# Gate panels moved in behind each head of a linear-attention stage, level scores computed in half the columns, and a weight ring of three

## The chip, the cores and the metric

The kernel runs on one core of a Trainium2 chip. The metric is the device time of one execution in microseconds (us), the median of several runs. The engines are named as in the profile: PE is TensorE's matrix multiplication and PEld its weight loads, DVE is VectorE, ACT is ScalarE, POOL is GpSimd, and SP is the queue that issues the transfers.

## What is computed

Three transformer-like layers over 512 positions of width 1024, all in float32. The first layer is the one that the change touches. Cut to what matters:

```python
proj = rmsnorm(x, norm_mix) @ w_in
zu, zv, zq, zf, zi, zo, g_a, g_b = jnp.split(proj, split_points, axis=-1)
y_a = gmlp_branch(zu, zv, ...) @ w_up_a          # GELU(u) * (W_s LN(GELU(v)) + b)
y_b = hgrn2_branch(zq, zf, zi, zo, ...) @ w_up_b # gated linear attention, 8 heads of 128
mix = sigmoid(g_a) * y_a + sigmoid(g_b) * y_b
x = x + mix @ w_out
x = x + square(relu(rmsnorm(x) @ w_ff1)) @ w_ff2
```

Inside `hgrn2_branch` each head needs, within every chunk, the scores of query t and key s with a decay between them: `scores = einsum('bhtk,bhsk,bhtsk->bhts', qb, kb, decay)` for s <= t. Then follow a short-convolution layer with its feed-forward block (`ffn_0`), keys and values, attention with 16 heads and a forget bias, and a second feed-forward block (`ffn_1`).

## The kernel before

Every activation lies transposed, features on the 128 partitions and the 512 positions in the free dimension, in tiles of 128x512. Every weight matrix is cut into panels of 128 output features: 353 panels of 128x1024 floats, in one long list whose order is `COUNTS` (L32): zu, zv (4 each), ga (8), upa (8), heads (32), gb (8), upb (8), out1 (8), ff1 (64), and so on. `START` holds where each name begins.

**A panel's way.** SP loads panel p into `w_raw`. ACT rounds it into `w_hi` (`high`, L400, a CAST), POOL subtracts the two into `w_lo` (`low`, L317), and PE multiplies (`product`, L1269): three matmuls of 512 columns for each of eight 128-row tiles (L1284, L1285, L1286: high times high, high times low, low times high), 24 in all, summed in bank p % 2 of PSUM. DVE takes the bank out (mostly `scale_out`, L786). The three buffers are rings of `RING` = 4 panels. ACT issues the rounding three panels ahead of the product that it stands beside (`p + 3`), and both ACT and POOL wait until the product that used the same ring place is made (`made`). A product waits for its `w_low` and for the eviction of the panel two before it.

**Order.** Each engine's program is written out by hand; engines meet through semaphores alone. The gMLP branch comes first: zu, zv, then the eight ga panels with the transposes of zv (`turn_zv`, L1308) and the layer norm (`layer_norm`, L843) beside them, then the mixing matmuls (L1324), then the eight upa panels, which have only four 128-row tiles each (12 matmuls). Then come the heads, then gb, upb, out1.

**A head.** `head(h, a)` stands once on each engine, and works on the four panels of head h (forget, query, value, output gate) and on the attention of head a = h - 1. On PE (L1392) the four products are cut in halves, and between them lie `turns` (transposes and the diagonal products, L1330), `levels` (four calls), `chunk_kv`, `outputs`, and at the end `output_sums` (L1388), which waits until ACT has squared the outputs (L528). The scores within a chunk are built level by level: seven levels, half lengths 64 to 1, each a product of the decayed tile `qk` with itself. `levels(c, a)` makes all seven 128x128 products of one chunk into two banks (L1361). DVE multiplies them and the diagonal by 0/1 masks (`mask_chunk`, L880, three instructions), and POOL adds the eight parts in three steps (`chunk_scores`, L330: L333, L335, L339), from one buffer `masked` that the four chunks share. DVE also forms the decays (`span`, L904, L914 and L915), ACT exponentiates them (L521, L525, L531), POOL multiplies the keys in (`decay_keys`, L342) and DVE the queries (`decay_queries`, L917, L922). Before the sums come the rounding of a panel or two on ACT and their subtraction on POOL.

Most repeated parts are hardware loops (`Fori`): heads 1 to 7, ff1, the convolution and feed-forward pairs, the attention pairs. Waits inside them compare a semaphore with a register, and in the attention loop the keys and values of the pair are copied to fixed places first (`k_now`, `v_now`), and DVE writes a mark (L1197) before each maximum.

Of the kernel before, what the change touches and what calls it, by code (L numbers as in the profile page):

```python
# [8 lines left out]
P = 128  # L9
# [18 lines left out]
ARENA = 17424  # L28


RING = 4
COUNTS = [("zu", 4), ("zv", 4), ("ga", 8), ("upa", 8), ("heads", 32), ("gb", 8), ("upb", 8), ("out1", 8),  # L32
          ("ff1", 64), ("conv_b", 8), ("conv_ch", 16), ("out2", 8), ("ffn_0", 68), ("k", 8), ("v", 8),
          ("f", 1), ("qg", 16), ("out3", 8), ("ffn_1", 68)]
START, N_PANELS = {}, 0
for _name, _n in COUNTS:
    START[_name] = N_PANELS
    N_PANELS += _n
# [4 lines left out]
for _name, _n in [("ident", P), ("ones", P), ("halves", P), ("minus", P), ("neg", P), ("reset", SEQ),  # L43
                  ("levels", LEVELS * P), ("onehot", HEADS_A), ("eps", 1)]:
    CONST_COLS[_name] = (_at, _n)
    _at += _n
# [16 lines left out]
HID_GMLP, HID_HEADS, HID_MIX, HID_FF1, HID_CONV, HID_FFN0, HID_ATTN, HID_FFN1 = 0, 4, 12, 20, 52, 60, 82, 90  # L63


class Steps:

    def __init__(self, eng, sem):  # L70
        self.eng, self.sem, self.n, self.offset = eng, sem, 0, 0
# [6 lines left out]
    def wait(self):  # L78
        self.eng.wait_ge(self.sem, self.n + self.offset)

    @contextmanager
    def loop(self, first, end, marks):
        before = self.n
        with self.eng.Fori(first, end) as i:
            self.offset = (i - first) * marks
            yield i
        self.offset = 0
        assert self.n - before == marks, f"the body marks {self.n - before} steps, not {marks}"
        self.n = before + (end - first) * marks


def tile_at(buf, i):

    if isinstance(i, int):
        return buf[:, i, :]
    return buf[:, bass.ds(i, 1), :].rearrange("p a n -> p (a n)")


def column(buf, i, rows=P):
    return buf[0:rows, i:i + 1] if isinstance(i, int) else buf[0:rows, bass.ds(i, 1)]  # L100


def build(nc, xT, panels, const, param, rows, ws, outT):
# [5 lines left out]
    with ctx:  # L109
# [16 lines left out]
        hid_lo = sb("hid_lo", [P, DT, SEQ], R)  # L126
        consts = sb("consts", [P, N_CONST])
# [3 lines left out]
        wait_mark = sb("wait_mark", [P, 1])  # L131
# [8 lines left out]
        def gain(name, i=0):  # L140
            a, _ = PARAM_COLS[name]
            return column(params, a + i)
# [3 lines left out]
        def take(*shape):  # L146
# [18 lines left out]
        zu, zv = take(GROUPS, SEQ), take(GROUPS, SEQ)  # L165
        vn = take(BLK, SEQ)
        rows_sb = take(3, SEQ)
        ws_sb = take(GROUPS, P)
        ln_stats, ln_mv = take(BLK, 6), take(BLK, 2)
        ln_root, ln_inv = take(BLK), take(BLK)  # L170

        used[0] = after_y
        qk = take(2 + LEVELS, SEQ)
        masked = take(LEVELS + 1, P)

        at = used[0]
        z, za, g, cum = take(SEQ), take(SEQ), take(SEQ), take(SEQ)
        q, k, vT, silu_o = take(SEQ), take(SEQ), take(SEQ), take(SEQ)
        gb = arena[:, at:used[0]].rearrange("p (a n) -> p a n", a=DT)
# [33 lines left out]
        k_now, v_now, key_bias, o_all = take(SEQ), take(SEQ), take(SEQ), take(SEQ)  # L213
# [19 lines left out]
        dve_steps, act_steps, pool_steps = sem("dve_steps"), sem("act_steps"), sem("pool_steps")  # L233
# [10 lines left out]
        level_made, level_masked, scores_done, kv_made, states_done = (sem(n) for n in (  # L244
            "level_made", "level_masked", "scores_done", "kv_made", "states_done"))
# [7 lines left out]
        k_squared, k_normed, v_copied, v_flat, v_spread = (sem(n) for n in (  # L253
            "k_squared", "k_normed", "v_copied", "v_flat", "v_spread"))
        l_abs, l_log, l_done, picked, biased, bias_read = (sem(n) for n in (
            "l_abs", "l_log", "l_done", "picked", "biased", "bias_read"))
        k_loaded, v_loaded, scored, maxed, exped, scaled, turned_p, copied_even, copied_odd, attended, attn_read = (sem(n) for n in (
            "k_loaded", "v_loaded", "scored", "maxed", "exped", "scaled", "turned_p", "copied_even", "copied_odd", "attended", "attn_read"))
# [16 lines left out]
        def _(sp):  # L275
            def load(i, j):
                sp.dma_start(w_raw[:, j, :], panels[i * RING + j]).then_inc(w_in[j], 16)

            sp.dma_start(params[:], param).then_inc(param_in, 16)
            for m in range(DT):  # L280
                sp.dma_start(x[:, m, :], xT[m]).then_inc(x_in[m], 16)
                if m == 0:
                    load(0, 0)
            load(0, 1)
            sp.dma_start(consts[:], const).then_inc(c_in, 16)
            for j in range(2, RING):
                load(0, j)
            sp.dma_start(rows_sb[:, :, :], rows.partition_broadcast(P)).then_inc(row_in, 16)
            sp.dma_start(ws_sb[:, :, :], ws).then_inc(row_in, 16)
            with sp.Fori(1, N_PANELS // RING) as i:  # L290
                at = sp.snap(i * RING)
                for j in range(RING):
                    src = panels[bass.ds(at + j, 1)].rearrange("a p n -> p (a n)")

                    sp.wait_ge(w_low, i * RING + (j - RING + 1))
                    sp.dma_start(w_raw[:, j, :], src).then_inc(w_in[j], 16)
# [1400 lines left out]
```

## Time and profile before

| | |
|---|---|
| runs | 2279.59, 2282.51, 2283.90 us; median 2282.51 us |
| the profiled execution | span 2280.2 us, 28102 instructions |
| DVE, ACT and POOL busy | 1053.0, 803.4 and 1023.1 us |
| idle of PE before L1292 | 55.1 us, 46.7 of them ended by ACT L528 |
| transfers | 353 panels of 512 KB, 3.5 us to land each; 84 GB/s on average |

The profiled execution is 2.3 us shorter than the median of the runs: the span counts from the first to the last instruction. A busy row says how long an engine had something in it. The chain of the page follows the work that ended last backwards, from each instruction to what released it. A window of the trace gives each engine's busy time between two moments counted from the start of the span, with the clock that TensorE was granted as a share of its full 2.4 GHz. Windows below begin at the first matmul of a stage's first product.

### The profile page before, as it was taken

How to read it: one execution, taken by the hardware profiler on the slowest of the kernel's cores; microseconds unless marked ns; L12 is line 12 of the kernel's file. 1: busy time of each engine (PE TensorE's matmuls, PEld its weight loads, DVE VectorE, ACT ScalarE, POOL GpSimd, SP SyncE). 2: the span in 40 equal slices, each digit the busy share in tenths (PEclk: the TensorE clock that was granted, in tenths of full speed). 3: DMA queues.
4: the chain of work that ended last, by engine and by line, in shares of the span. 5: the costliest groups of instructions: out<-in, count | busy, mean ns of one | idle time of the engine just before them, and what ended most of it. 6: DMA issues, size and time to landing. Idle time of an engine off the chain costs nothing.

```text
span 2280.2 us, 28102 instructions
## 1 busy us (share of the span) xinstructions
PE 2178.6 (96%) x9662; PEld 1748.7 (77%) x9662; DVE 1053.0 (46%) x1683; ACT 803.4 (35%) x1141; POOL 1023.1 (45%) x517
## 2 busy tenths in 40 slices
PE   6988887889999999999999999999899999999999
PEld 5876766778788888888788888877666668888887
DVE  3348888862432232434455252531455444625343
ACT  4334435433422222532332222253455544222222
POOL 3457777774344444444444444453311113444443
PEclk9999998999999999999999999999899999999999
DMA  5231111123233332232333233332211002232322
GB/s 186 93 111 47 46 55 46 46 65 93 93 93 94 100 101 92 92 102 84 101 93 101 93 97 97 92 115 80 74 37 36 29 28 93 92 103 91 102 92 93
DMA packets 53779, 192.44 MB, mean 84 GB/s; under 512 B 5968, under 2 KB 6096, under 8 KB 53584
## 3 DMA queue, kind: packets, MB, share of 16 engines
q1 hardware_dynamic: 53712, 191.51, 26.7%
q8 instruction: 46, 0.75, 0.1%
q14 instruction: 21, 0.17, 0.0%
HBM read 189.39 MB, written 2.10 MB: 84 GB/s over the span
## 4 chain that ended last, share of the span: by engine, by line
PE 81%; DVE 9%; issue 4%; POOL 3%; ACT 2%; DMA 0%; SPq 0%; POOLq 0%; DVEq 0%; ACTq 0%
PE ps L1284 25%; PE ps L1286 25%; PE ps L1285 25%; DVE arena L914 2%; PE ps L1515 2%; PE ps L1538 2%; POOL arena L333 2%; POOL w_lo L317 1%; PE ps L1292 1%; DVE arena L915 1%; DVE arena L786 1%; DVE arena L922 1%; DVE arena L908 1%; DVE arena L1117 0%; PE ps L1517 0%
## 5 line engine op out<-in xcount | busy, mean ns | idle before, releaser
L317 POOL TENSOR_TENSOR w_lo<-w_raw,w_hi 128x1024 fp32r<-128x1024 f32 x353 | 851.1, 2413 | 1167.7 <-ACT w_hi L400 1154.9
L1284 PE MATMUL ps<-x_hi,w_hi 128*128 128x512 f32 x1864 | 758.2, 407 | 17.9 <-POOL w_lo L317 9.3
L1285 PE MATMUL ps<-x_lo,w_hi 128*128 128x512 f32 x1864 | 735.0, 394 | 0.0
L1286 PE MATMUL ps<-x_hi,w_lo 128*128 128x512 f32 x1864 | 734.9, 394 | 0.0
L400 ACT CAST w_hi<-w_raw 128x1024 fp32r<-128x1024 f32 x353 | 366.5, 1040 | 346.6 <-PE ps L1286 345.1
L1284 PEld LDWEIGHTS ps<-x_hi,w_hi 128*128 128x128 f32 x1864 | 357.1, 192 | 99.3 <-issue 14.2
L1285 PEld LDWEIGHTS ps<-x_lo,w_hi 128*128 128x128 f32 x1864 | 356.9, 191 | 81.7 <-issue 9.4
L1286 PEld LDWEIGHTS ps<-x_hi,w_lo 128*128 128x128 f32 x1864 | 355.5, 191 | 76.4
L786 DVE TENSOR_TENSOR arena<-ps,inv_rms 128x512 f32<-128x512 f32 x232 | 160.0, 690 | 479.2 <-PE ps L1286 455.6
L1284 PE MATMUL ps<-hid_hi,w_hi 128*128 128x512 f32 x896 | 354.2, 395 | 13.5 <-DVE hid_lo L815 13.2
L1285 PE MATMUL ps<-hid_lo,w_hi 128*128 128x512 f32 x896 | 351.9, 393 | 0.0
L1286 PE MATMUL ps<-hid_hi,w_lo 128*128 128x512 f32 x896 | 351.5, 392 | 0.0
L1284 PEld LDWEIGHTS ps<-hid_hi,w_hi 128*128 128x128 f32 x896 | 170.2, 190 | 53.5 <-DVE hid_lo L815 15.3
L409 ACT ACTIVATE hid_hi<-arena 128x512 fp32r<-128x512 f32 (+1 forms) x112 | 70.0, 631 | 385.0 <-DVE arena L1117 136.8
L1286 PEld LDWEIGHTS ps<-hid_hi,w_lo 128*128 128x128 f32 x896 | 170.2, 190 | 35.9
L1285 PEld LDWEIGHTS ps<-hid_lo,w_hi 128*128 128x128 f32 x896 | 170.5, 190 | 35.1
L815 DVE TENSOR_TENSOR hid_lo<-arena,hid_hi 128x512 fp32r<-128x512 f32 (+1 forms) x112 | 79.2, 712 | 77.4 <-ACT hid_hi L409 77.3
L1134 DVE TENSOR_TENSOR x<-x,ps 128x512 f32<-128x512 f32 x40 | 27.5, 687 | 162.4 <-PE ps L1286 162.4
L643 ACT ACTIVATE arena<-arena 128x512 f32<-128x512 f32 x44 | 27.8, 632 | 211.2 <-DVE arena L1083 211.2
L1292 PE MATMUL ps<-arena,consts 128*128 128x512 f32 x62 | 39.9, 732 | 55.1 <-ACT arena L528 46.7
L1117 DVE TENSOR_TENSOR arena<-arena 128x512 f32<-128x512 f32 x44 | 82.7, 1880 | 4.3
L352 POOL TENSOR_TENSOR arena<-arena 128x256 f32<-128x256 f32 x56 | 63.4, 1164 | 26.5 <-ACT arena L525 26.5
(159 smaller groups left out, 1678.1 us busy)
## 6 DMA issues: line engine op xcount, KB each, us to landing
w_raw<-in_panels SPq DMA_DIRECT2D x353, 512.0 KB, 3.5
x<-in_xT SPq DMA_DIRECT2D x8, 256.0 KB, 4.9
outT<-x SPq DMA_DIRECT2D x8, 256.0 KB, 2.0
consts<-in_const SPq DMA_DIRECT2D x1, 1032.5 KB, 8.4
arena<-in_rows SPq DMA_DIRECT2D x1, 768.0 KB, 11.1
arena<-in_ws SPq DMA_DIRECT2D x1, 256.0 KB, 11.4
params<-in_param SPq DMA_DIRECT2D x1, 112.0 KB, 2.1
```

The lines of the kernel that those rows point to most:

```text
L317: nc.gpsimd.tensor_tensor(w_lo[:, j, :], w_raw[:, j, :], w_hi[:, j, :].bitcast(F), ALU.subtract).then_inc(w_low, 1)
L333: steps.done(nc.gpsimd.tensor_tensor(masked[:, 0:4, :], masked[:, 0:4, :], masked[:, 4:8, :], ALU.add))
L352: nc.gpsimd.tensor_tensor(lv, lv, kv, ALU.mult).then_inc(keys_decayed, 1)
L400: nc.scalar.copy(w_hi[:, j, :], w_raw[:, j, :]).then_inc(w_high, 1)
L409: return nc.scalar.activation(dst, src, ACT.Copy, scale=1.0 if scale is None else scale)
L786: return v.tensor_tensor(dst, bank(p_int), inv_rms[:, :], ALU.mult)
L815: v.tensor_tensor(tile_at(hid_lo, m), src, tile_at(hid_hi, m).bitcast(F), ALU.subtract).then_inc(hid_low, 1)
L1117: v.tensor_tensor(conv_o[:, j, :], conv_u[:, j, :], conv_t[:, j, :], ALU.mult).then_inc(hid_raw, 1)
L1284: nc.tensor.matmul(o, wh, hi[:, kt, :], start=(kt == 0), stop=False)
L1285: nc.tensor.matmul(o, wh, lo[:, kt, :], start=False, stop=False)
L1286: ins = nc.tensor.matmul(o, wl, hi[:, kt, :], start=False, stop=(kt == tiles - 1))
L1292: nc.tensor.matmul(ps[:, bank_n, :], weights, src, start=True, stop=True).then_inc(sums_ready, 1)
```

## The change

- **Loops written out.** No `Fori` is left; all waits are on constants. `k_now`, `v_now` with their copies and waits, and the mark before each maximum, go.
- **Order of the panels.** The eight ga panels and the eight gb panels no longer stand before and behind the heads. `FILL` puts two panels behind the four of heads 1 to 4, one behind heads 5 and 6, two behind head 7, and the last four gb panels are the products of the pass that finishes head 7. upa follows after the heads.
- **The gMLP work** (transposes, layer norm, mixing) moves into head 0, its rounding (`split_gmlp`, `low_gmlp`) into head 1, into buffers of its own (`gm_hi`, `gm_lo`). Before the first turns PE waits until DVE has read the mixed tiles. The sigmoids of ga and gb move to upa and upb.
- **Level scores.** A call of `levels` makes one group of levels for all four chunks, and only the columns of the later halves: 64 instead of 128 moving columns. The number of matmuls stays at 28 a head. DVE copies them into `scores` (cleared once), the first level plainly, the others and the diagonal under a mask with `copy_predicated`: eight copies and four marker instructions a head. POOL's twelve additions a head go, and so do the twelve mask multiplications.
- **Ring of three**, with `FEED` = 2: rounding and subtraction run two panels ahead. The memory freed holds the new buffers; gb lies in `x`, which is loaded again during upb.
- `silu_o` has two buffers, and its eviction comes ahead of the gating of the head before it.

```diff
+RING = 3
+FEED = 2
+FILL = {1: [("ga", 0), ("ga", 1)], 2: [("ga", 2), ("ga", 3)], 3: [("ga", 4), ("ga", 5)],
+        4: [("ga", 6), ("ga", 7)], 5: [("gb", 0)], 6: [("gb", 1)], 7: [("gb", 2), ("gb", 3)],
+        8: [("gb", 4), ("gb", 5), ("gb", 6), ("gb", 7)]}
...
+            for h in range(HEADS_H):
+                p = AT["heads", 4 * h]
+                low(p + 2)
+                low(p + 3)
+                pool.wait_ge(decays_done, h * 4 + 1)
+                decay_keys(h, [0])
+                low(p + 4)
+                pool.wait_ge(decays_done, h * 4 + 2)
+                decay_keys(h, [1, 2, 3, 4])
+                low(p + 5)
+                pool.wait_ge(decays_done, h * 4 + 3)
+                decay_keys(h, [5, 6, 7])
+                for e in range(len(FILL.get(h, []))):
+                    low(p + 6 + e)
...
+            def take_levels(gr, a):
...
+                for at, n in enumerate(LEVEL_GROUPS[gr]):
...
+                    if n == 0:
+                        ins = v.tensor_copy(scores[0:half, :, half:P],
+                                            got[0:half, :].rearrange("p (b n) -> p b n", b=BLK))
+                    else:
...
+                        ins = v.copy_predicated(dst, mask.unsqueeze(1).broadcast_to([P, BLK, P // (2 * half), half]),
+                                                got.rearrange("p (b s h) -> p b s h", b=BLK, h=half))
+                    link(ins)
...
+                v.engine_nop().then_inc(level_taken, 1)
...
+                        ins = nc.tensor.matmul(ps[0:rows_, 4 + gr % 2, to:to + P // 2], lv[:, 0:rows_], later,
+                                               start=True, stop=True)
...
             def turns(a):
...
+                if a > 0:
                     pe.wait_ge(sums_read, a + (R_HEAD))
+                else:
+                    pe.wait_ge(mixed_read, GROUPS)
...
             def head(h, a):
...
+                if h == 0:
+                    for b in range(BLK):
+                        turn_zv(b)
...
+                if h == 0:
+                    mix()
+                fill = FILL.get(h, []) if h is not None else []
+                if fill:
+                    product(p + 4, x_hi, x_lo)
                 if a is not None:
                     output_sums(a)
...
+                for e in range(1, len(fill)):
+                    product(p + 4 + e, x_hi, x_lo)
```

## Rows read from the trace of the kernel before

**Rows 1.** The page: busy time, share of the span and instructions of each engine.
```profile
PE 2178.6 (96%) x9662; PEld 1748.7 (77%) x9662; DVE 1053.0 (46%) x1683; ACT 803.4 (35%) x1141; POOL 1023.1 (45%) x517
```

**Rows 2.** The page's chain of work that ended last, by engine.
```profile
PE 81%; DVE 9%; issue 4%; POOL 3%; ACT 2%; DMA 0%; SPq 0%; POOLq 0%; DVEq 0%; ACTq 0%
```

**Rows 3.** Windows: ga, upa, heads, gb, ff1, attention; PE, PEld, DVE, ACT, POOL, clock, DMA.
```profile
68.09:119.75 51.66, 49.37 (x241) 41.09 (x240) 22.51 (x33) 16.91 (x22) 19.43 (x8) 1.00 0.29 92
119.75:149.28 29.53, 25.02 (x97) 19.43 (x98) 10.62 (x16) 11.48 (x12) 18.13 (x8) 0.88 0.37 108
149.28:475.57 326.29, 272.67 (x1420) 225.54 (x1419) 268.08 (x389) 144.23 (x201) 234.71 (x175) 0.92 0.17 55
475.57:532.61 57.04, 57.04 (x288) 47.83 (x286) 21.60 (x37) 21.98 (x32) 35.87 (x27) 0.97 0.21 65
...
623.65:972.72 349.07, 349.07 (x1539) 288.68 (x1538) 104.35 (x151) 105.89 (x129) 151.53 (x65) 1.00 0.31 97
...
1622.42:1851.77 229.35, 223.69 (x862) 143.70 (x863) 119.15 (x410) 121.91 (x257) 40.09 (x17) 0.95 0.12 39
```

**Rows 4.** Windows: head 0, and head 5, one of seven alike.
```profile
149.28:174.28 25.00, 21.92 (x98) 17.83 (x96) 14.94 (x19) 10.09 (x14) 12.16 (x6) 1.00 0.35 107
...
347.48:389.93 42.45, 35.33 (x192) 29.30 (x190) 36.16 (x54) 19.07 (x28) 31.59 (x25) 0.94 0.16 49
```

**Rows 5.** Timeline of PE in head 5, between the products; last, after its wait.
```profile
354.39 0.60 PE L1335 MATMUL ps<-consts,arena 128*128 128x128 f32 x4
...
360.37 1.73 PE L1361 MATMUL ps<-arena 128*128 128x128 f32 x14
...
388.84 2.08 PE L1292 MATMUL ps<-arena,consts 128*128 128x512 f32 x2 [6.67 <-ACT arena L528]
```

**Rows 6.** A window right behind that wait.
```profile
390.50:396.50 6.00, 6.00 (x20) 4.63 (x19) 5.82 (x7) 3.32 (x7) 5.79 (x7) 0.70 0.00 0
```

**Rows 7.** Timeline of DVE in head 5.
```profile
359.80 1.65 DVE L937 TENSOR_TENSOR arena<-arena 128x512 f32<-128x512 f32 x1
...
378.85 2.60 DVE L914 TENSOR_TENSOR arena<-arena 128x256 f32<-128x256 f32 x1
...
385.61 0.41 DVE L914 TENSOR_TENSOR arena<-arena 128x256 f32<-128x256 f32 x1
```

**Rows 8.** Timeline of POOL in head 5.
```profile
359.24 1.66 POOL L333 TENSOR_TENSOR arena<-arena 128x512 f32<-128x512 f32 x1 [0.63 <-DVE arena L890]
...
378.61 2.56 POOL L317 TENSOR_TENSOR w_lo<-w_raw,w_hi 128x1024 fp32r<-128x1024 f32 x1
...
388.38 7.91 POOL L352 TENSOR_TENSOR arena<-arena 128x256 f32<-128x256 f32 x7 [3.31 <-ACT arena L525]
```

**Rows 9.** Groups of DVE's instructions by line and shape, 149.28 to 510.40.
```profile
L914 DVE TENSOR_TENSOR arena<-arena 128x256 f32<-128x256 f32 x56 | 59.3, 1059 | 0.0
...
L886 DVE TENSOR_TENSOR arena<-ps,consts 128x512 f32<-128x512 f32 x32 | 21.9, 684 | 51.7 <-POOL arena L339 31.3 <-PE ps L1361 20.4
L888 DVE TENSOR_TENSOR arena<-ps,consts 128x384 f32<-128x384 f32 x32 | 17.5, 545 | 0.0
...
L890 DVE TENSOR_TENSOR arena<-ps,consts 128x128 f32<-128x128 f32 x32 | 8.9, 278 | 0.0
```

**Rows 10.** Timeline of the weight loads in attention, at full clock.
```profile
1711.25 0.29 PEld L1515 LDWEIGHTS ps<-arena 64*128 64x128 f32 x2 [0.76 <-issue]
```

**Rows 11.** Timeline at panel v 3: POOL's subtraction, PE's first matmul.
```profile
1577.27 2.40 POOL L317 TENSOR_TENSOR w_lo<-w_raw,w_hi 128x1024 fp32r<-128x1024 f32 x1 [8.66 <-ACT w_hi L400]
...
1581.21 0.48 PE L1284 MATMUL ps<-x_hi,w_hi 128*128 128x512 f32 x1
```

**Rows 12.** Timeline of DVE and PE at the layer norm and the mixing.
```profile
112.73 2.04 DVE L847 TENSOR_TENSOR arena<-arena 128x512 f32<-128x512 f32 x1
...
115.63 3.81 PE L1324 MATMUL ps<-arena 128*128 128x128 f32 x32 [1.99 <-DVE arena L848]
```

**Rows 13.** Timeline of ACT behind the last head.
```profile
514.55 1.28 ACT L554 ACT_TABLE_LOAD   x1
```

More of the change, by code:

```diff
@@ L78, in wait @@
     def wait(self):
[L79 to L100, printed above, removed]
+        self.eng.wait_ge(self.sem, self.n)
 def build(nc, xT, panels, const, param, rows, ws, outT):
@@ L1119, in pair @@
                         low_hid(m + (hid0 + t0 + 1), m, conv_o[:, j, :])
-                    pair(0, 0)
-                    pair(1, 1)
-                    with steps.loop(1, size // 2, 4) as i:
-                        for j in range(2):
-                            pair(i * 2 + j, j)
                     p0 += 2 * size
@@ L1268, in _, with product @@
         def _(pe):
-            def product(p, p_int, hi, lo, tiles=DT, ready=None, done=None, part=None):
-                j = p_int % RING
+            def product(p, hi, lo, tiles=DT, ready=None, done=None, part=None):
+                j = p % RING
                 part = part or (0, tiles)
@@ L1301, in linear @@
                 for m in range(n):
-                    product(p0 + m, p0 + m, hi, lo, tiles, ready if m == 0 else None, done)
+                    product(p0 + m, hi, lo, tiles, ready if m == 0 else None, done)
                     if m == 0 and stream is not None:
@@ L1392, in head @@
             def head(h, a):
-                p, p4 = S["heads"] + 4 * h if h is not None else S["gb"], S["heads"]
-                product(p, p4, x_hi, x_lo)
+                p = AT["heads", 4 * h] if h is not None else AT["gb", 4]
+                product(p, x_hi, x_lo)
+                if h == 0:
+                    for b in range(BLK):
+                        turn_zv(b)
                 if a is not None:
@@ L1413, in head @@
                     outputs(a)
-                product(p + 3, p4 + 3, x_hi, x_lo, part=(4, DT))
+                product(p + 3, x_hi, x_lo, part=(4, DT))
+                if h == 0:
+                    mix()
+                fill = FILL.get(h, []) if h is not None else []
+                if fill:
+                    product(p + 4, x_hi, x_lo)
                 if a is not None:
                     output_sums(a)
-            head(0, None)
-            with pe.Fori(1, HEADS_H) as h:
-                head(h, h - 1)
+                for e in range(1, len(fill)):
+                    product(p + 4 + e, x_hi, x_lo)
@@ L1422, in _ @@
+            for h in range(HEADS_H):
+                head(h, h - 1 if h > 0 else None)
             head(None, HEADS_H - 1)
[L1423 removed]
+            linear(S["upa"], DT, gm_hi, gm_lo, gm_low, 0, tiles=GROUPS)
             linear(S["upb"], DT, hid_hi, hid_lo, hid_low, HID_HEADS)
             linear(S["out1"], DT, hid_hi, hid_lo, hid_low, HID_MIX)
[L1428 removed]
+            for ch in range(FF1_CHUNKS):
                 p0 = S["ff1"] + 16 * ch
[L1430 to L1436 removed]
@@ L1447, in _ @@
                     sums(6, c("ones"), sum_sq_2[:, :])
[L1448 to L1450 removed]
+            linear(S["conv_ch"], 2 * DT, x_hi, x_lo, None, None)
             linear(S["out2"], DT, hid_hi, hid_lo, hid_low, HID_CONV)
```

734 lines of the change are left out of this document (322 added, 412 removed).

## Prediction

> **What bounds the kernel now.** I read the page first. PE is busy 96% of the span [rows 1]; the chain that ended last runs through PE for 81% and through DVE for 9% [rows 2]. So most of the kernel is PE at its pace, and the question is where it is not. The windows by stage answer that [rows 3]. In ff1 64 panels take 349.07 us, 5.45 each; I use 5.44, the pitch from product to product in a quiet stretch, as the price of a full panel. Four hardware loop edges lie in or beside that stage and PE is never idle in it. The heads, 32 panels, take 326.29 us where 32 x 5.44 would be 174; attention takes 229.35 for 16. For the change the stretch from ga to gb counts: 51.66 + 29.53 + 326.29 + 57.04 = 464.5 us.
>
> A head takes 42.45 us with PE busy 35.33 and DVE busy 36.16 [rows 4], and seven heads look alike (42.3 to 43.8). PE stands for 6.67 us before the sums, waiting for ACT L528 [rows 5], which waits for DVE's spans. Behind that wait the granted clock of the window is 0.70 [rows 6]: part of it at the lower level, 1.2 GHz, after 6.67 us in which PE did nothing; product 389.93 spans about 2.5 us more than one at full clock. So the heads are bound by DVE, with POOL and ACT in turn with it, and PE has room there.
>
> Why DVE is that full: its L914 takes 0.41 us alone, but 2.60 while POOL's L317 runs, and both end together; L937 takes 1.65 beside POOL's L333, again ending with it [rows 7, 8]. L914's 56 instructions sum to 59.3 us, where 56 x 0.41 would be 23 [rows 9]. An instruction of DVE with two inputs from on-chip memory waits for POOL's to end. Taking all lines of the heads so, about 11 of DVE's 36 us a head are such waits, and DVE alone would need 25. The Trainium skill ("SBUF — State Buffer", on who interferes with whom) says the same as an exclusive lock in which the loser fully blocks; the common end times here agree. That rule speaks against this change, which hangs one or two more of POOL's subtractions on each head; the third rival prices it from the rows.
>
> **The change part by part.**
>
> *PE's own work in a head.* Four products 21.8; seven transposes, and four diagonal products of two instructions each, all at 0.11, 0.8 + 0.9; levels 28 x 2 instructions at 0.11 (14 in 1.73 us, the last one's own 0.28 taken off, is 0.112) = 6.2; chunk_kv 0.7; outputs 1.5; sums 0.9; changeovers about 0.5. Sum 33.3 us [rows 5].
>
> *Level scores at 64 columns.* The count of matmuls stays, so the price per instruction decides. The trace has no matmul of 64 columns. Two weight loads of 0.18 us each start 0.11 us apart [rows 10], and the transposes of L1335, single instructions where L1361 has two for one product, also come at 0.11 (4 in 0.60) [rows 5]. That looks like a floor set by the weight load, not by the columns streamed. Bounds: nothing saved, or half, 3.1 us a head. I take nothing. In a sentence of its own: the Trainium skill ("TensorE: Matmul & The Clock Gate", LDWEIGHTS) prices a load by its columns, 128 / 1.2 = 107 ns, whatever is streamed behind it, which would give the same zero, against 25 us over eight heads if the streamed columns ruled; the 0.11 us start to start agrees.
>
> *DVE and POOL in a head.* Out go the twelve mask products: L886 0.68, L888 0.55, L890 0.28, four times, 5.4 us with their overlap taken off [rows 9]; and twelve additions on POOL, about 12 us. In come eight copies. The nearest rows are the mask products, which read the same memory: 0.68 for 512 columns, and 0.42 for 256, midway between 0.28 for 128 and 0.55 for 384 [rows 9]: 7 x 0.42 + 0.68 = 3.6, plus 0.1 of waiting behind each = 4.5. A masked copy isn't in the trace; if it took twice the time per element it would be 3.6 more. DVE's waits behind the vanished additions (L937, L944, L964, L908) were 3.4. Each fill panel adds an eviction of 0.7 and a subtraction of 2.4 that can block DVE for up to 2.2. DVE: 36.2 - 5.4 + 4.5 - 3.4 = 31.9, with one fill 33 to 35, with two 34 to 38.
>
> *Fill panels.* PE then needs 33.3 + 5.44 = 38.7 us with one, 44.2 with two. I laid the four queues beside each other with the durations above. With PE's first product at 0, the last levels end at 22; DVE's q, spans and evictions run to 30 to 32; the output squares are done by 31, before PE comes to the sums at 38, since the first fill product now lies where it stood idle; POOL finishes the keys at 40 to 42 and the next head's levels want them at 46 (one fill) or 51 (two). The tightest points are the subtraction of the panel after next (done 36.5 to 38.5, wanted at 38.7 with one fill, 41 to 43 against 44.2 with two) and silu_o's eviction (35 to 37.6 against 38.7). So PE becomes the bound and its clock stays at 2.4 GHz; I add 0.5 us a head for those points. Heads 1 to 7 with twelve fills: 7 x 33.8 + 12 x 5.44 = 301.9 us.
>
> *Head 0* took 25.00 [rows 4] and now carries the gMLP. DVE's statistics 3.6, four norms of 2.2 with one or two blocked like L847 (2.04 for 0.69) [rows 12] 10, before it may evict panel 1, at 23 us; PE wants to start panel 3 at 18, idle 5. Then mixing, 3.6 [rows 12], to 34, the next product to 39.5; but the first turns now wait for the mixed tiles to be read, and those reads (4 x 1.4) stand on DVE behind spans, queries and evictions, done at 46 to 48. Another 7 us idle, and after each stall some time at half clock, 3 us in all. Head 0 costs 45 us (40 to 52).
>
> *The last pass* (gb 4 to 7 and head 7): 34 us. *upa* behind it: 8 x 2.73 = 21.8, plus a wait for its third panel: the rounding stands behind root, gating, split, a table load of 1.28 [rows 13] and a sigmoid, done about 9.5 us after the sums where PE wants it at 5.5: 25.8 us. Bounds 22 to 31.
>
> *Sum.* 45 + 301.9 + 34 + 25.8 = 406.7 against 464.5: 57.8 us less.
>
> *Ring of three, feed of two*, everywhere else. `high(p + 2)` with a ring of three waits for the same product as `high(p + 3)` with a ring of four, and stands at the same place of ACT's queue. So every rounding, subtraction and load keeps its moment and serves a panel one earlier: the margin of a panel is its start less the end of the subtraction now made for the panel behind it. I took that for all panels. It is 1.54 us in v (1577.27 + 2.40 against 1581.21) [rows 11], about the smallest there is outside the stretch already costed; it is never negative there. Cost nothing; if loads or POOL fell 2 us later, half a microsecond for each of some 60 panels, 30 us.
>
> *Loads of x again* on SP hold a panel's load until an eviction, about 2.5 us, with over 5 us to spare: nothing. *Attention*: PE is busy 223.69 of 229.35 [rows 3], so what goes from ACT and DVE (two copies a pair, 64 marks) was hidden: nothing, bounds -6 to 0. *Loops*: ff1 shows no idle time at their edges: nothing, bounds -5 to +10 for the longer code.
>
> Against the profiled execution: 2280.2 - 57.8 = 2222.4; the median lies 2.3 above the span, so 2224.7, say 2225 us.
>
> **The rivals.** (1) The forecast, PE bounds the heads: 2225, its own range 2212 to 2238. (2) The 64 columns do save: 25 us, of which DVE lets about 20 through: 2205. For: nothing but the column count; against: [rows 10]. (3) Slower: DVE and POOL take turns fully. DVE alone 25.5 and POOL 6 x 2.4 + 1.5 + 7 x 0.75 = 21.2 (seven took 7.91 beside DVE [rows 8], 1.13 each, of which about 0.4 was DVE's turn) are 47 us with two fills, 44 with one; with the 6 us that DVE now idles for others, 53 and 50, so 5 x 53 + 2 x 50 = 365, 63 us more than forecast: 2288; with masked copies at double price 2317. I take 2300. It decides once heads 1 to 7 average over 51.4 us, (301.9 + 57.8) / 7. Against: POOL's and DVE's busy times overlap now for most of a head, 36.16 + 31.59 in 42.45 [rows 4]. (4) The tail of a head misses its tight points by 3 to 4 us each: 25 more, 2250. For: margins of 0 to 2 us. (5) The ring starves later stages: 2255. (6) The longer code stalls its engines: the change is not what it says; 2240. (7) Head 0 and attention give more than I grant: 2195.
>
> **How the numbers follow.** Chances: (1) 0.50, (2) 0.14, (3) 0.06, (4) 0.17, (5) 0.05, (6) 0.03, (7) 0.05. The predicted time is that of (1). The range 2198 to 2256 takes in (2), (4), (5) and (6), leaving out (3), (7) and the ends of (4). A measurement of this kernel can tell about 0.2%, 4.6 us, from no change. Slower by more than that is (3) and what I may have overlooked, 0.07; within it 0.03, from a (3) or (4) that meets the old time; faster 0.90.
>
> **What the profile after would show.** Heads 1 to 4 near 44 us and 5 and 6 near 39, clock 1.0, no wait above 1 us before the sums; L1361's successor at 0.11 us per instruction; head 0 near 45 with two stalls of 5 and 7 us; DVE below 38 us a head; subtractions ending before their products everywhere else. It would be wrong if the fills show idle time behind POOL's subtraction or DVE's eviction, if a masked copy takes well over 0.5 us, or if v and the feed-forward stages leave 5.44 us a panel.

## The result and the profile after

The changed kernel takes 2240.56 us (median; runs 2239.78 to 2241.88) where the kernel before took 2282.26 beside it. The ratio is 0.9819, 95% interval 0.9805 to 0.9833: 41.7 us less, where 57.8 were forecast. The time lies within the range on record, 15.6 us above the predicted 2225. Span to span it is 2280.2 to 2238.0, 42.2 us.

Some short names are used below. The *stretch* is ga, upa, heads and gb together, 464.5 us before; in the changed kernel it runs from head 0 to the end of upa. A *fill* is a gate panel whose product stands behind the four products of a head. The *sums* are the two matmuls of `output_sums`, the *spans*, *queries* and *keys* are the instructions of `span` and `decay_queries` on DVE and of `decay_keys` on POOL, and an *eviction* is DVE's copy of a finished product out of PSUM.

Page of the changed kernel, its busy row and its chain by engine (before: [rows 1, 2]), and its group of PE's first matmuls of a product: busy time, mean, idle time before them and what ended it.

```profile
PE 2166.2 (97%) x9662; PEld 1742.7 (78%) x9662; DVE 971.8 (43%) x1588; ACT 792.0 (35%) x1123; POOL 930.7 (42%) x421
...
PE 83%; issue 7%; DVE 4%; POOL 4%; ACT 1%; DMA 0%; SPq 0%; DVEq 0%; POOLq 0%
...
L1215 PE MATMUL ps<-x_hi,w_hi 128*128 128x512 f32 x1864 | 752.0, 403 | 38.0 <-POOL w_lo L304 21.6
```

DVE lost 81 us of work and POOL 92, as the change says. But PE still stands 38 us before the first matmuls of products, 21.6 of them for POOL's subtraction. Windows of the changed kernel, columns as in [rows 3]: head 0, head 1, head 3 and head 5 (two fills and one), the last pass, upa.

```profile
65.04:99.91 34.87, 29.60 (x146) 24.69 (x144) 27.10 (x40) 12.58 (x18) 8.69 (x4) 0.90 0.15 52
99.91:161.30 61.39, 47.69 (x238) 39.98 (x239) 51.78 (x76) 28.40 (x40) 37.06 (x22) 0.89 0.17 57
209.01:256.73 47.72, 45.67 (x239) 38.28 (x237) 31.15 (x50) 21.23 (x29) 24.61 (x15) 0.96 0.20 66
304.43:344.97 40.54, 38.48 (x215) 32.54 (x213) 28.66 (x48) 18.53 (x26) 17.44 (x11) 1.00 0.18 62
433.50:466.11 32.61, 32.61 (x191) 28.17 (x190) 9.79 (x18) 6.29 (x8) 11.81 (x5) 1.00 0.30 98
466.11:493.47 27.36, 23.92 (x99) 19.16 (x97) 7.38 (x11) 16.17 (x21) 17.95 (x8) 0.94 0.36 121
```

The stretch that was 464.5 us is now 493.47 - 65.04 = 428.4: 36.1 less. The start is 3.05 shorter (head 0 begins at 65.04, ga began at 68.09 [rows 3]), the stages behind the stretch together 3.1.

What PE waited for in the stretch, from 65 to 480 us (total, times, longest):

```profile
PE ps L1215 <- POOL w_lo L304: 15.8, 7, 3.4
PE ps L1215 <- DVE arena L701: 10.9, 2, 5.6
PE ps L1264 <- DVE x L784: 8.1, 1, 8.1
```

Six of the seven POOL waits are the same one, once in each of heads 2 to 7: 2.05 us before the product behind the sums (the seventh is upa's, 3.44). Where a head has two fills this product is the second fill; where it has one, it is the next head's first panel. The timelines of PE and POOL in head 3 show it; columns: start, duration, what, count, idle time before and its releaser.

```profile
246.46 1.02 PE L1223 MATMUL ps<-arena,consts 128*128 128x512 f32 x2
249.53 0.50 PE L1215 MATMUL ps<-x_hi,w_hi 128*128 128x512 f32 x1 [2.05 <-POOL w_lo L304]
...
250.20 0.63 PE L1217 MATMUL ps<-x_hi,w_lo 128*128 128x512 f32 x1
```

```profile
235.63 2.54 POOL L304 TENSOR_TENSOR w_lo<-w_raw,w_hi 128x1024 fp32r<-128x1024 f32 x1
241.50 5.15 POOL L317 TENSOR_TENSOR arena<-arena 128x256 f32<-128x256 f32 x4 [3.33 <-ACT arena L460]
246.61 2.87 POOL L304 TENSOR_TENSOR w_lo<-w_raw,w_hi 128x1024 fp32r<-128x1024 f32 x1
```

POOL stood idle for 3.33 us, multiplied four keys, and only then made the subtraction that PE wanted. ACT had finished the rounding for it at 235.27, and POOL was free from 238.17. Behind the stall the matmuls take 0.63 us instead of 0.39; the window right behind it has a granted clock of 0.72, partly 1.2 GHz. The same stall at the end of head 6 left the clock at 1.00 (second line):

```profile
249.48:255.48 6.00, 5.95 (x19) 4.73 (x20) 2.58 (x3) 2.77 (x4) 6.00 (x5) 0.72 0.23 87
...
387.23:393.23 6.00, 6.00 (x28) 4.96 (x29) 2.67 (x4) 2.73 (x4) 6.00 (x5) 1.00 0.26 87
```

Of the six stalls four were followed by a fall of the clock (heads 2 to 5) and two were not (heads 6 and 7).

### The profile page after: what moved, and what is told of

Same layout as the page of the kernel before. It is cut to its first block, busy times and chain, and to the rows that moved or that the text cites. A ratio compares the mean times of both kernels' runs of the same rounds, so it can differ in the third digit from the quotient of the medians.

```text
span 2238.0 us, 24392 instructions
## 1 busy us (share of the span) xinstructions
PE 2166.2 (97%) x9662; PEld 1742.7 (78%) x9662; DVE 971.8 (43%) x1588; ACT 792.0 (35%) x1123; POOL 930.7 (42%) x421
## 4 chain that ended last, share of the span: by engine, by line
PE 83%; issue 7%; DVE 4%; POOL 4%; ACT 1%; DMA 0%; SPq 0%; DVEq 0%; POOLq 0%
PE ps L1215 26%; PE ps L1217 25%; PE ps L1216 25%; POOL w_lo L304 2%; PE ps L1443 2%; PE ps L1466 2%; POOL arena L317 2%; PE ps L1223 1%; PE ps L1295 1%; PE ps L1445 0%; PE ps L1474 0%; PE ps L1457 0%; POOL arena L312 0%; DVE arena L843 0%; DVE arena L844 0%
## 5 line engine op out<-in xcount | busy, mean ns | idle before, releaser
L1215 PE MATMUL ps<-x_hi,w_hi 128*128 128x512 f32 x1864 | 752.0, 403 | 38.0 <-POOL w_lo L304 21.6
L701 DVE TENSOR_TENSOR arena<-ps,inv_rms 128x512 f32<-128x512 f32 x216 | 149.0, 690 | 493.1 <-PE ps L1217 473.4
L1215 PE MATMUL ps<-hid_hi,w_hi 128*128 128x512 f32 x864 | 338.4, 392 | 5.4 <-DVE hid_lo L730 5.3
L1216 PE MATMUL ps<-hid_lo,w_hi 128*128 128x512 f32 x864 | 337.5, 391 | 0.0
L1217 PE MATMUL ps<-hid_hi,w_lo 128*128 128x512 f32 x864 | 337.4, 391 | 0.0
L1215 PEld LDWEIGHTS ps<-hid_hi,w_hi 128*128 128x128 f32 x864 | 162.9, 188 | 41.1 <-DVE hid_lo L730 4.7
L353 ACT ACTIVATE hid_hi<-arena 128x512 fp32r<-128x512 f32 x108 | 67.6, 632 | 358.0 <-DVE arena L1058 134.7
L1216 PEld LDWEIGHTS ps<-hid_lo,w_hi 128*128 128x128 f32 x864 | 163.0, 189 | 33.7
L730 DVE TENSOR_TENSOR hid_lo<-arena,hid_hi 128x512 fp32r<-128x512 f32 x108 | 78.3, 730 | 69.9 <-ACT hid_hi L353 69.9
L1070 DVE TENSOR_TENSOR x<-x,ps 128x512 f32<-128x512 f32 x40 | 27.5, 688 | 166.2 <-PE ps L1217 166.2
L317 POOL TENSOR_TENSOR arena<-arena 128x256 f32<-128x256 f32 x56 | 64.9, 1187 | 26.6 <-ACT arena L460 26.6
L994 DVE TENSOR_TENSOR x<-x,ps 128x512 f32<-128x512 f32 x24 | 16.5, 688 | 107.7 <-PE ps L1217 107.7
L1058 DVE TENSOR_TENSOR arena<-arena 128x512 f32<-128x512 f32 x44 | 62.4, 1419 | 1.5
```

The lines of the kernel that those rows point to most:

```text
L317: nc.gpsimd.tensor_tensor(lv, lv, kv, ALU.mult).then_inc(keys_decayed, 1)
L353: return nc.scalar.activation(dst, src, ACT.Copy, scale=1.0 if scale is None else scale)
L701: return v.tensor_tensor(dst, bank(p), inv_rms[:, :], ALU.mult)
L730: v.tensor_tensor(hid_lo[:, m, :], src, hid_hi[:, m, :].bitcast(F), ALU.subtract).then_inc(hid_low, 1)
L1058: v.tensor_tensor(conv_o[:, j, :], conv_u[:, j, :], conv_t[:, j, :], ALU.mult).then_inc(hid_raw, 1)
L1215: nc.tensor.matmul(o, wh, hi[:, kt, :], start=(kt == 0), stop=False)
```

## The experiments

**1. POOL's order, one line.**

```diff
                 low(p + 4)
+                low(p + 5)
                 pool.wait_ge(decays_done, h * 4 + 2)
                 decay_keys(h, [1, 2, 3, 4])
-                low(p + 5)
```

> The changed kernel with one line of POOL moved: the subtraction low(p + 5) stands directly behind low(p + 4), ahead of the wait for the second batch of decays and of decay_keys 1 to 4, instead of behind them. Theory A (order on POOL): in every head from 1 on PE stands 2.05 us for this subtraction before a product, and the product then runs partly at a granted clock below 1 (7.2 us instead of 5.44). The rounding it needs is ready 10 us earlier, so the stall goes and the clock stays: heads 2 to 4 47.7 -> 43.8 us, 5 and 6 about 2 to 4 less, 7 46.3 -> 43; total 24 to 28 us less, about 2214 us. Theory B (DVE's chain bounds the head after all, POOL only shows it): the subtraction now blocks DVE's spans for 2.4 us, the keys come as much later, and PE waits in the next head before its first levels; heads stay within 1 us of 47.7, total 2236 to 2242 us.

Measured: 2232.4 us (ratio to before 0.9783, 0.9767 to 0.9799), heads 45.6 with two fills, 40.1 with one. The total is 18 us above theory A's. The 2.05 us stall went, but another of 1.24 us came, before the first fill, for DVE's eviction of the third panel. Timelines of DVE and POOL in head 3:

```profile
236.50 2.58 DVE L843 TENSOR_TENSOR arena<-arena 128x256 f32<-128x256 f32 x1
239.01 2.62 DVE L844 TENSOR_TENSOR arena<-arena 128x256 f32<-128x256 f32 x1
...
242.22 0.68 DVE L701 TENSOR_TENSOR arena<-ps,inv_rms 128x512 f32<-128x512 f32 x1
```

```profile
236.26 5.09 POOL L304 TENSOR_TENSOR w_lo<-w_raw,w_hi 128x1024 fp32r<-128x1024 f32 x2
```

Two subtractions back to back held up two spans: they took 2.6 us each instead of 0.41, and the eviction behind them came later. Neither theory as written: the order on POOL was the cause, and the block of DVE that theory B named took back part of the gain, at another place.

**2. 128 streamed columns again.** The level products of three chunks in four stream the whole tile instead of the later halves. The expectation says that the output stays the same. It does not: the tile is streamed in order, so the 64 columns that remain of it are not the later halves, and these scores are not the reference's. Which instructions run, and their shapes, do not depend on the values, so the times are still used here.

```diff
+                        if b < BLK - 1:
+                            ins = nc.tensor.matmul(ps[0:rows_, 4 + gr % 2, to:to + P], lv[:, 0:rows_], lv,
+                                                   start=True, stop=True)
+                            continue
```

> The changed kernel, but three of every four level products stream 128 columns again instead of 64 (the surplus half is overwritten by the next product, the output stays the same); the stationary columns are as in the change. Theory A (the stationary columns set the pace): the starts of successive level products stay where they are, 0.112 us apart with 128 stationary columns and 0.058 with 64; total unchanged within 1 us of 2240.6. Theory B (streamed columns count): 42 of 56 instructions a head get 0.03 to 0.05 us slower, 1.2 to 2.2 us a head, total 2250 to 2258 us.

Measured: 2243.0 us (2239.6 to 2243.8; ratio to before 0.9825), 2.4 us above the changed kernel where theory A allowed 1 and theory B 10 or more. Heads 2 and 4 took 48.0 and 48.1, 0.3 to 0.4 more than in the changed kernel, and head 3 took 46.45. Timeline of PE at the first group of head 3: stationary by partitions "128*64", then what is streamed.

```profile
217.93 0.87 PE L1296 MATMUL ps<-arena 128*64 128x128 f32 x6
218.64 0.28 PE L1299 MATMUL ps<-arena 128*64 128x64 f32 x2
218.84 0.94 PE L1296 MATMUL ps<-arena 128*128 128x128 f32 x6
```

Where 64 columns are stationary, six instructions with 128 streamed take 218.64 - 217.93 = 0.71 us, 0.118 each. In the changed kernel, with 64 streamed, by line and shape in head 3 (count, busy us, mean ns):

```profile
L1295 PE MATMUL ps<-arena 128*128 128x64 f32 x48 | 5.9, 272 | 0.0
...
L1295 PE MATMUL ps<-arena 128*64 128x64 f32 x8 | 0.7, 228 | 0.0
```

Single instructions tell it apart better. Past the first two of a group they start, at full clock in these two heads, 0.058 us apart with 64 stationary and 64 streamed, 0.109 with 64 stationary and 128 streamed, 0.112 with 128 stationary and 64 streamed, and 0.111 with 128 on both sides. So in these four cases the longer of the two sides sets the pace. Theory A holds for six levels of seven, but not for the first, which it had at its short pace with 128 streamed. The halves save where both sides are short: eight of 56 instructions, 8 x (0.111 - 0.058) = 0.4 us a head.

**3. The old scores in the new order.** Masked products on DVE and additions on POOL as before (mask_chunk and chunk_scores of the kernel before); order, fills, ring and unrolled loops of the change.

> The changed kernel with one part undone: the scores are made as before, by chunks of seven full products, three masked products on DVE and three additions on POOL for each chunk; order, fills, ring, written-out loops stay as changed (two gate panels change places, so that the masked products find room, and the masks are bf16). Theory A (the compact scores make the room that the fills use): DVE gets 4 to 5 us a head more and POOL 12 us more, in front of its subtractions; heads 2 to 4 go from 47.7 to 52 us or more, total 2270 to 2300 us. Theory B (the new order alone brings the gain, DVE and POOL have room for the old scores once PE has work while it waited): heads 47 to 49 us, total 2240 to 2252 us.

Measured: 2267.1 us (0.9934, 0.9917 to 0.9951), 26.6 us above the changed kernel. Heads 2 to 4 took 52.5, 50.9 and 51.0. Head 3:

```profile
219.42:270.36 50.94, 46.58 (x238) 38.50 (x237) 36.89 (x54) 21.07 (x29) 35.54 (x27) 0.97 0.18 61
```

DVE has 5.7 us more and POOL 10.9 more than in head 3 of the changed kernel; in heads 2 to 7 PE waits 2.8 us for an eviction, and in heads 2 to 6 1.1 to 2.8 for a subtraction. This is theory A's mechanism, with two of the three heads 1 us short of its 52 and the total 3 us under its range. Everything in the change except the compact scores (order, ring, written-out loops) is worth 14.7 us against the kernel before (2281.8 beside this run); the compact scores give the other 27. In this run's profile (a slower execution than its median, 2269.9) the stretch took 458.25 us, 6.3 less than before, and the rest of the kernel 5.8 less. So within the stretch the new order with the old scores gains little. The reverse, compact scores in the old order, was not run, and how much they give alone is not known.

**4. Fills in head 0**, with the line of the first experiment and the rounding of the gMLP out of head 1.

```diff
+FILL = {0: [("ga", 0), ("ga", 1)], 1: [("ga", 2)], 2: [("ga", 3), ("ga", 4)], ...
...
+                    if 1 <= a <= GROUPS:
+                        low_gmlp(a - 1)
```

> The changed kernel with the POOL line moved as in the run with low(p + 5) earlier, and two things more. The four low_gmlp subtractions of DVE leave the end of head 1, where they keep an eviction waiting and PE stands 5.61 us, for the ends of heads 2 to 5. Head 0 takes two gate panels, so that PE has work while DVE reads the mixed tiles (it stood 8.09 us for them in head 1), and DVE evicts its second and third panel before and behind the four norms instead of behind them (PE stood 5.26 us). Theory A: heads 0 and 1 with three gate panels end at about 148 us of the span instead of 161.3 with two; with the heads' gain the total is 2194 to 2202 us. Theory B (DVE's own 45 us of head 0 set the end of the pair, whatever PE is given): the pair ends at 155 us or later, total 2203 to 2210 us.

Measured: 2222.1 us (0.9738, 0.9721 to 0.9754). Head 2 began at 158.6, as theory B has it. The total is 12 us above its range: the later heads kept the 45.7 and 40.1 us of the first experiment, more time than either theory had counted on. PE stood 3.42 us for the subtraction of the first fill, which waited behind key 0 although its rounding was done, and 6.91 for the eviction of the fourth panel, behind DVE's spans and queries. The stall for low_gmlp (in the changed kernel four subtractions of DVE, 6.34 us, before an eviction) was gone:

```profile
146.81 6.34 DVE L793 TENSOR_TENSOR gm_lo<-x,gm_hi 128x512 fp32r<-128x512 f32 x4
153.07 0.68 DVE L701 TENSOR_TENSOR arena<-ps,inv_rms 128x512 f32<-128x512 f32 x1
```

**5. Both subtractions earlier.**

```diff
+                low(p + 4)
                 pool.wait_ge(decays_done, h * 4 + 1)
                 decay_keys(h, [0])
-                low(p + 4)
+                low(p + 5)
                 pool.wait_ge(decays_done, h * 4 + 2)
                 decay_keys(h, [1, 2, 3, 4])
-                low(p + 5)
```

> The changed kernel with POOL's order in a head: low(p + 4) ahead of decay_keys 0 instead of behind it, low(p + 5) ahead of decay_keys 1 to 4 instead of behind them. In the run with only the second of these moves the 2.05 us stall went, but two subtractions then stood back to back beside DVE's spans, two spans took 2.6 us instead of 0.41, and the eviction behind them came 1.24 us late for the first gate panel. Theory A (DVE is blocked once per subtraction of POOL that runs beside its spans): low(p + 4) now runs 5 us earlier, where DVE waits for PE, one span is blocked instead of two, the eviction is 2.2 us earlier and the stall of 1.24 us goes: heads 2 to 4 45.7 -> 43.5 to 44.2 us, 5 and 6 40.1 -> 38 to 38.7, total 2217 to 2223 us. Theory B (DVE's eviction is late by its own chain, which starts behind the last level scores): heads stay at 45.5, total 2230 to 2234 us.

Measured: 2223.85 us (0.9744, 0.9727 to 0.9760), theory A, with the total 0.9 us above its range. Windows of head 3 (two fills) and head 5 (one):

```profile
207.30:251.10 43.80, 43.80 (x239) 37.25 (x237) 32.09 (x50) 21.15 (x30) 24.07 (x14) 1.00 0.25 73
294.90:332.81 37.91, 37.91 (x215) 32.59 (x213) 27.67 (x47) 17.68 (x24) 19.11 (x11) 1.00 0.27 84
```

PE is busy throughout, at full clock, and in heads 2 to 7 it waits nowhere. These heads are PE's own work, and the forecast's sums for it were 44.2 and 38.7. Head 1, which carries the gMLP's rounding, still took 62.4.

**6. Everything so far, and the third panel evicted behind the first span.**

> The changed kernel with everything that the runs so far point to: POOL's two subtractions ahead of the keys; DVE evicts the third panel of a head behind its first span; low_gmlp behind heads 2 to 5; head 0 takes two gate panels, evicts its second and third panel around the norms and its fourth before the later spans; the multiplications of gmlp_out go from head 0 to DVE's wait at the start of head 1. Theory A: heads 2 to 7 at 43.5 to 44 us with two gate panels and 38.2 with one, the first product of head 2 at 150 us of the span (158.6 in the run with the earlier fills, three gate panels each), total 2198 to 2206 us. Theory B (head 0 stays bound by DVE's norms, spans and additions): head 2 starts at 156 us or later and the total is 2207 us or more.

Measured: 2227.6 us (0.9756), worse than with POOL's order alone (experiment 5). Head 2 began at 156.0 and the total is 2207 or more, as theory B has both, but its reason covers head 0 alone; the larger loss lies in the later heads. Heads 2 and 3 went back to 47.9 and 47.8, with 2.16 us before the product behind the sums in each head from 1 to 7, now for DVE's eviction of the fourth panel. Seven queries on DVE and seven keys on POOL, here in step:

```profile
237.28 6.48 DVE L854 TENSOR_TENSOR arena<-arena 128x256 f32<-128x256 f32 x7
```

```profile
237.26 6.23 POOL L317 TENSOR_TENSOR arena<-arena 128x256 f32<-128x256 f32 x7 [4.33 <-ACT arena L460]
```

and in the run before, where POOL began half a microsecond ahead of DVE:

```profile
240.30 1.42 DVE L851 TENSOR_TENSOR arena<-arena 128x256 f32<-128x256 f32 x4
241.94 2.43 DVE L851 TENSOR_TENSOR arena<-arena 128x256 f32<-128x256 f32 x3 [0.22 <-ACT arena L466]
```

```profile
239.80 8.00 POOL L317 TENSOR_TENSOR arena<-arena 128x256 f32<-128x256 f32 x7 [3.32 <-ACT arena L460]
```

The same fourteen instructions: when they start together (POOL 0.02 to 0.03 us ahead) they take turns and DVE pays; when POOL starts 0.5 us ahead it pays. The first of its seven keys then took 2.52 us by itself, while the rest of DVE's spans and four of its queries passed at 0.41 each:

```profile
239.80 2.52 POOL L317 TENSOR_TENSOR arena<-arena 128x256 f32<-128x256 f32 x1 [3.32 <-ACT arena L460]
```

This is not one head's accident. In this run the seven queries took 6.5 us in all seven heads in which POOL was 0.02 to 0.03 ahead; in experiment 5 they took 4.1 in all seven heads in which it was 0.5 ahead. Only DVE has an eviction behind them.

**7. The start and the attention.** One subtraction of POOL more before that of the third panel; ACT's two copies a pair in the attention.

> The changed kernel with two additions in stages that do not touch one another. First, in the start POOL does one subtraction more (128 x 1024, its result unused) before that of the third panel, so that two stand beside DVE's first sums of squares, as with the ring of four. Theory A (the ring of three lets the first root come earlier, since DVE's sums wait for one subtraction less): the seven sums take 9.6 us instead of 7.5 and head 0 starts 2 to 3 us later, near 68. Theory B (the smaller constants or loads bring the earlier start): it stays at 65 to 66 us. Second, in the attention ACT copies a tile of v and one of k per pair again (results unused), where they stood before. Theory A (their removal is worth nothing or moves work into a clash): qg takes 229 to 231 us, as now. Theory B (they were hidden by nothing else and had cost time): qg 234 us or more.

Measured: 2242.6 us, 2.05 above the changed kernel. Head 0 starts at 68.07: theory A. DVE's seven sums with POOL beside them, here and in the changed kernel:

```profile
17.11 9.37 DVE L718 TENSOR_TENSOR arena<-arena 128x512 f32<-128x512 f32 x7
```

```profile
16.37 7.48 DVE L712 TENSOR_TENSOR arena<-arena 128x512 f32<-128x512 f32 x7
```

In the kernel before, with a ring of four, the same seven and POOL's two subtractions beside them:

```profile
16.41 9.59 DVE L797 TENSOR_TENSOR arena<-arena 128x512 f32<-128x512 f32 x7
```

```profile
18.77 5.09 POOL L317 TENSOR_TENSOR w_lo<-w_raw,w_hi 128x1024 fp32r<-128x1024 f32 x2 [3.35 <-ACT w_hi L400]
```

The added subtraction does not account for the whole 3.03 us by which head 0 starts later than at 65.04. The seven sums took 1.89 us longer and PE waited 2.16 longer behind them, but in this execution the very first product had also begun 0.72 later (10.03 against 9.31), before the addition could matter. Over the nine profiles with a ring of three and no such addition head 0 starts between 64.5 and 66.8.

Attention: 230.98 us, no difference: the copies had been hidden.

**8. The attention's marks as well.** The copies, and a memset before each row maximum.

> The changed kernel with the attention's removed work put back, its results unused: ACT's two copies a pair and the small memset of DVE in front of each of the 64 row maxima. The copies alone left qg at 230.98 us, where the changed kernel has 230.96 and the kernel before 229.36. Theory A (the marks shift DVE's turns against POOL's so that less of them meets): qg back at 229.4 us. Theory B (the 1.6 us come from elsewhere, the ring or the written-out loop): 230.9 us or more.

Measured: 2240.4 us (two runs only), attention 231.3: theory B. The 1.6 us that the attention lost are not what was removed from it.

**9. A version that beats both.** Experiment 5's order; head 0 as in experiment 6; the spans as in the change; in head 0 the next head's subtraction ahead of keys 5 to 7.

```diff
+                if h == 0:
+                    low(p + 6)
                 pool.wait_ge(decays_done, h * 4 + 3)
                 decay_keys(h, [5, 6, 7])
```

> The changed kernel with POOL's two subtractions ahead of the keys as in the run that moved both; low_gmlp behind heads 2 to 5; head 0 with two gate panels, its second and third panel evicted around the norms, its fourth ahead of the later spans, the multiplications of gmlp_out in head 1; and, new, in head 0 the subtraction of head 1's first panel ahead of decay_keys 5 to 7 (PE waited 5.86 us for it). DVE's spans in heads 1 to 7 keep the order of the change: with the third panel evicted behind the first span DVE's seven queries ran in step with POOL's seven keys, 6.5 us instead of 4.07, and PE waited 2.16 us in every head. Theory A: heads 43.8 and 38 us again, head 2 starts at 149 to 153 us with three gate panels made; total 2200 to 2207 us. Theory B (the queries fall in step with the keys here too, since low_gmlp and the fills shift DVE): heads 46 to 48 us, total 2215 us or more.

Measured: 2200.9 us (0.9640, 0.9627 to 0.9653), theory A. Heads 43.8 to 44.3 and 37.9 to 38.4, head 2 from 151.86. What PE still waited for between 65 and 500 us:

```profile
PE ps L1230 <- POOL w_lo L304: 7.0, 2, 3.6
PE ps L1230 <- DVE arena L703: 1.4, 2, 0.9
PE ps L1268 <- DVE arena L767: 1.1, 1, 1.1
```

## Why the prediction was right, and where it was off

**The mechanism** held in its direction: the room behind DVE's chain was filled with products, DVE and POOL lost the score work, and PE came close to bounding the heads (busy 45.67 of 47.72 us in head 3). The time, though, is outside the forecast's own range of 2212 to 2238 and lies between it (1) and its rival (4), a tail of the head that misses its tight points. By mechanism it is rival (4): 2.05 us of waiting in each of heads 2 to 7, which cost 2.0 to 3.9 us a head with what the clock took, where the rival had 3 to 4. The prediction's own sign of being wrong, idle time behind POOL's subtraction in the fills, is there. That 2240.6 meets rival (6), longer code that stalls its engines (2240), is a coincidence: the instructions fell from 28102 to 24392, and attention is the only stage behind the stretch that grew by more than 0.1 us.

**Part of the nearness is luck.** The sum covered the stretch, 406.7 us; it took 428.4, so the sum missed by 21.7 us and not by 15.6. The other 6.1 came from stages whose change was put at nothing: 3.05 at the start and 3.06 behind the stretch.

**The step that failed** is the timing of the tight points in a head, first of all the subtraction of the panel after next: "done 36.5 to 38.5, wanted at 38.7". In head 3 it was wanted at 247.48 - 209.01 = 38.5 and done at 249.48 - 209.01 = 40.5. I had it 2 to 4 us too early, because the four keys ahead of it start at 32.5 and take 5.15. And I read the margin wrongly with two fills: 44.2 is when the second fill ends, but the panel after next is the second fill itself and is wanted when the first ends. My allowance of 0.5 us a head for all tight points should have been 2.0 to 3.9. Experiment 5 takes the stall away, and heads 3 and 5 take 43.80 and 37.91 instead of 47.72 and 40.54.

**PE's own work**, 44.2 and 38.7: right within 0.8 us, by the same run. The first level's 64 columns are 0.4 us of it.

**Heads, by the sum.** Heads 2 to 4 took 47.7 each against 44.7, 5 and 6 40.5 and 42.3 against 39.2, 7 46.3 against 44.7: together 14.9 us of the miss. Last pass 32.6 against 34, upa 27.4 against 25.8, its wait of 3.44 for the third panel as described.

**Head 0 and 1**: 96.3 us against 89.7. The two stalls forecast at 5 and 7 us measured 5.26 and 8.09; the miss is a third one that the sum does not contain, 5.61 us in head 1, where `low_gmlp` stands ahead of silu_o's eviction and takes 6.34 beside POOL. The sum has no term for these four, so it left out instructions that the change moves.

**DVE and POOL.** DVE is busy 31.2 us in a head with two fills, below the 34 to 38 forecast. The masked copies are not the reason. Those of 256 columns took 0.55 us on average, 0.45 for four of a head's six and 0.75 for the two finest levels, and one of 512 took 0.76, against 0.42 and 0.68 taken from the mask products; a head's eight copies took 4.4 us against 3.6. What fell is DVE's blocked time: the 112 instructions of the spans took 92.8 us in the kernel before (59.3 in L914 [rows 9], 33.5 in L915) and 72.9 in the changed one (40.7 and 32.2), 2.5 less a head.

```profile
218.47 0.45 DVE L811 COPY_PREDICATED arena<-consts,ps 128x256 f32<-128x256 int32 x1
...
L811 DVE COPY_PREDICATED arena<-consts,ps 128x256 f32<-128x256 int32 x48 | 26.2, 545 | 24.1 <-PE ps L1295 23.2
...
223.46 0.76 DVE L816 COPY_PREDICATED arena<-consts,ps 128x512 f32<-128x512 int32 x1
```

The rival of full turn-taking (3) did not come: heads of 47.7, not 53. But the two engines did block each other. The Trainium skill ("SBUF — State Buffer", who interferes with whom) has the loser of the shared port block until the winner ends; the spans of 2.58 and 2.62 us in experiment 1 agree. The blocking decided where the stall stood, not whether the heads were bound. The prediction told it one-sidedly, as DVE waiting for POOL: in experiment 5 it was POOL's first key that waited, 2.52 us. Its reading that both "end together" is also rough: in [rows 7, 8] L914 ends at 381.45 and POOL at 381.17, L937 at 361.45 and POOL at 360.90. DVE ends 0.28 and 0.55 us later, somewhat less than these instructions take alone (0.41 and 0.69), which fits one that waits for POOL's end and then runs.

**Levels at 64 columns** were taken at nothing: nearly so. Rival (2), 25 us, is out by experiment 2, where undoing three quarters of it cost 0.3 to 0.4 us a head. The Trainium skill ("TensorE: Matmul & The Clock Gate", LDWEIGHTS) prices a load by its columns; the first level, with 64 stationary columns, agrees as long as 64 are streamed (0.058 us). With 128 streamed it ran at 0.109 to 0.118 us, which the load's price alone would not give.

**The ring of three** cost nothing, as forecast: out1, ff1, the convolution, k and v kept their lengths within 0.1 us (ff1 349.07 both times). But I missed what it gives: of the 3 us at the start about 2 (2.16 in experiment 7), since one of POOL's subtractions no longer stands beside DVE's first sums.

**Loops**: forecast nothing, bounds -5 to +10; ffn_0 and ffn_1 are 1.6 and 1.9 us shorter and out2 0.6, in single panels at places where a loop began or ended, and out3 is 0.7 shorter. No run isolates it. **Attention**: forecast -6 to 0, measured +1.6, where the window

```profile
1581.25:1812.21 230.96, 225.10 (x863) 144.01 (x863) 117.26 (x351) 113.81 (x242) 40.19 (x17) 0.94 0.11 39
```

has a granted clock of 0.94 against 0.95 in [rows 3], and PE busy 1.4 us longer with the same work. It is not chance: the ten profiles of kernels with the written-out attention have 230.8 to 231.3 us. Unrounded the granted shares are 0.946 before and 0.941 after; share times length is 217.1 and 217.3 us, so 1.3 of the 1.6 goes with the clock. Why it is lower there stays open. Neither the copies nor the marks explain it.

## What to carry to other kernels

When an engine is meant to become the bound, list for each of its waits the one instruction that releases it, and look at what stands in front of that on its own in-order queue: here a subtraction whose input was ready eleven microseconds earlier, and whose engine was free eight earlier, stood behind work that was itself waiting. Moving two ready subtractions ahead of waits (experiment 5) gave 16.7 us, four tenths of what the whole change gave. Where two engines block each other, place the long instruction of the one where the other waits anyway, and check in a run which of them pays. And when work is moved between stages, give every moved instruction a term in the sum: the four that had none cost 5.6 us.

## What was unexpected of the hardware

- DVE's and POOL's short instructions interleave in more than one way: seven against seven took 6.48 (DVE) and 6.23 us (POOL) when they began together, and 1.42 + 2.43 and 8.00 when POOL began 0.5 us ahead. Where they began together PE then stood 2.16 us for DVE's eviction in every head. The order of other instructions differs too between these two runs, but the two outcomes go with the offset in every head of both.
- A stall of 2.05 us cost up to 3.9: head 3 had 47.72 us with it and 43.80 without. The clock did not fall behind every one: head 7 had the same stall at a granted clock of 1.00, 46.28 us against 44.25 without. In experiment 2 head 3 kept 1.00 with it and took 46.45 us, its neighbours 48.0 and 48.1.
- A matmul instruction with 64 stationary and 64 streamed columns follows its predecessor in about half the time of one with 128 on either side: 0.058 us against 0.109 to 0.112.
